# Two stretches of projections behind every second step of both attentions, in place of one behind each step

## The reference

```python
def first_block(x, ...):
    h = rms_norm(x, attn_norm)
    x = x + hybrid_mixer(h, ...)      # proj = h @ w_in: q_f, k_f, v_f, forget gate, q_s, k_s, v_s, two gates
    h = rms_norm(x, ffn_norm)
    x = x + hier_moe(h, ...)          # 64 experts, 2 per token
    return rms_norm(x, final_norm)

# hybrid_mixer: two attentions of 8 heads of 64 features
o_f = fox_attention(q_f, k_f, v_f, log_f)       # causal, plus cumulated log forget gates
o_s = swa_sink_attention(rotary(q_s), rotary(k_s), v_s, sinks)   # window of 128, one sink per head
merged = sigmoid(gl_f + b) * (o_f @ w_proj_fox) + sigmoid(gl_s + b) * (o_s @ w_proj_swa)
return merged @ w_out

# second_block, its mixer: retention of 4 heads and latent attention (MLA) of 8 heads, 96 features for q and k
ret_out = silu(rg) * head_groupnorm(retention(rq, rk, rv))
mla_out = mla_causal(q, k, v)
return concatenate([ret_out, mla_out]) @ w_o    # then the gated feed-forward of 2816 and the last gate
```

## Time and profile before

| what | us |
|---|---|
| median of 3 runs | 2106.96 (2105.54 to 2107.35) |
| the profiled execution | 2105.58 |
| its span, first to last instruction | 2103.8 |
| TensorE busy, whole span | 1805.8 (86%) |
| VectorE busy | 778.0 (37%) |
| ScalarE busy | 694.2 (33%) |
| mean granted clock | 0.95 |

### The profile page before, as it was taken

How to read it: one execution, slowest core, us unless ns; L and a number is a source line. 1 busy time by engine, 2 the same in 40 slices (tenths; PEclk the granted TensorE clock), 3 DMA queues, 4 the chain that set the end, 5 groups by cost and what they waited for, 6 DMA issues and landing times.

```text
span 2103.8 us, 35728 instructions
## 1 busy us (share of the span) xinstructions
PE 1805.8 (86%) x14374; PEld 1232.2 (59%) x14374; DVE 778.0 (37%) x1481; ACT 694.2 (33%) x1292; POOL 77.6 (4%) x184
## 2 busy tenths in 40 slices
PE   7999999787877768777877778699979899999988
PEld 5677787543434434343433434378757788788866
DVE  4555425632222222222222222445455633332254
ACT  4444422232222232223222232432555422222151
POOL 0000000000000000000000002410000000000000
PEclk9999999898999999999999999899989999999999
DMA  6222233599999999999999999742221132324211
GB/s 202 76 81 81 61 100 103 216 410 425 427 426 426 426 426 427 425 428 426 427 426 425 427 425 427 288 120 76 67 85 51 61 99 81 109 91 140 100 61 40
DMA packets 108451, 505.95 MB, mean 240 GB/s; under 512 B 9400, under 2 KB 58808, under 8 KB 75104
## 3 DMA queue, kind: packets, MB, share of 16 engines
q1 hardware_dynamic: 99744, 490.49, 58.4%
q10 hardware_dynamic: 7520, 11.37, 2.0%
q0 software_dynamic: 1120, 3.16, 0.5%
HBM read 497.31 MB, written 2.11 MB: 237 GB/s over the span
## 4 chain that ended last, share of the span: by engine, by line
PE 59%; DMA 29%; DVE 7%; ACT 3%; issue 2%; SPq 1%; ACTq 0%; DVEq 0%
DMA ring<-in_w 28%; PE bank L609 13%; PE bank L610 12%; PE bank L611 12%; PE bank L2131 8%; PE bank L2043 4%; PE bank L2122 3%; PE bank L773 2%; DVE w_lo L707 2%; ACT w_hi L694 1%; PE bank L799 1%; PE bank L785 1%; SPq L1716 1%; DMA raw<-in_w_in 1%; PE bank L1096 0%
## 5 line engine op out<-in xcount | busy, mean ns | idle before, releaser
L2131 PE MATMUL bank<-ring,XTs 128*32 128x256 f32 x4096 | 287.2, 428 | 113.9 <-DMA ring<-in_w 110.4
L2369 DVE TENSOR_TENSOR x<-x,bank 128x512 f32<-128x512 f32 x264 | 163.8, 681 | 486.5 <-PE bank L2122 486.5
L609 PE MATMUL bank<-hTh,w_hi 128*128 128x512 f32 x714 | 288.1, 404 | 13.5 <-DVE w_lo L707 6.7
L2131 PEld LDWEIGHTS bank<-ring,XTs 128*32 128x32 f32 x4096 | 142.8, 120 | 259.4 <-issue 201.5
L707 DVE TENSOR_TENSOR w_lo<-raw,w_hi 128x2048 fp32r<-128x2048 f32 (+3 forms) x85 | 183.1, 2158 | 299.2 <-ACT w_hi L694 299.1
L610 PE MATMUL bank<-hTh,w_lo 128*128 128x512 f32 x714 | 283.7, 397 | 0.0
L611 PE MATMUL bank<-hTl,w_hi 128*128 128x512 f32 x714 | 282.8, 396 | 0.0
L694 ACT ACTIVATE w_hi<-raw 128x2048 fp32r<-128x2048 f32 (+3 forms) x85 | 152.9, 1805 | 173.2 <-PE bank L611 170.3
L2140 PE MATMUL bank<-ring,aT 128*32 128x256 f32 x2048 | 126.9, 389 | 89.5 <-DVE aT L2389 89.5
L1918 ACT ACTIVATE y<-bank 32x256 f32<-32x256 f32 x256 | 95.9, 375 | 226.9 <-PE bank L2122 139.9
L609 PEld LDWEIGHTS bank<-hTh,w_hi 128*128 128x128 f32 x714 | 136.2, 191 | 55.5 <-DVE w_lo L707 17.6
(11 more groups left out here) (375 smaller groups left out, 2249.5 us busy)
## 6 DMA issues: line engine op xcount, KB each, us to landing
ring<-in_w SPq DMA_DIRECT2D x192, 2048.0 KB, 19.6
raw<-in_w_in SPq DMA_DIRECT2D x25, 1024.0 KB, 5.5
raw<-in_w_gate SPq DMA_DIRECT2D x11, 1024.0 KB, 5.3
raw<-in_w_up SPq DMA_DIRECT2D x11, 1024.0 KB, 5.3
raw<-in_w_down SPq DMA_DIRECT2D x11, 1024.0 KB, 4.9
raw<-in_w_out SPq DMA_DIRECT2D x4, 1024.0 KB, 5.1
raw<-in_w_o SPq DMA_DIRECT2D x4, 1024.0 KB, 5.2
raw<-in_w_ple_gate SPq DMA_DIRECT2D x4, 1024.0 KB, 5.1
```

The source lines that it names most:

```text
L609: pe.matmul(dst, left[0], right[0], start=start, stop=False)
L2131: mm = pe.matmul(Hb[BLK * j:BLK * (j + 1), :], XTs[u][:, 4 * (c % 2) + 2 * h + c // 2, :], w[:, at_:at_ + Q], start=(h == 0 and c == 0), s ...
L2369: ins = v.tensor_tensor(xs, xs, Sb[t % 2][n][:, :], ALU.add)
```

## The change

A helper `every_second` wraps a generator: `between(t)` takes nothing behind even steps and two stretches behind odd ones. All six calls use it, three engines in each attention. No instruction is added or taken away. What the steps and the generators issue is the same; the generator's rest is still drained behind the attention.

```diff
+        def every_second(stretches):
+
+            def between(t):
+                if t % 2:
+                    for _ in range(2):
+                        next(stretches, None)
+            return between
...
             stretches = pe_between()
-            pe_attention(pe, MLA, lambda t: next(stretches, None))
+            pe_attention(pe, MLA, every_second(stretches))
...
             stretches = dve_between()
-            dve_attention(v, MLA, chain, lambda t: next(stretches, None))
+            dve_attention(v, MLA, chain, every_second(stretches))
...
             stretches = act_between()
-            act_attention(act, MLA, lambda t: next(stretches, None))
+            act_attention(act, MLA, every_second(stretches))
...
             stretches = act_between()
-            act_attention(act, ATT, lambda t: next(stretches, None))
+            act_attention(act, ATT, every_second(stretches))
...
-            pe_attention(pe, ATT, lambda t: next(stretches, None))
+            pe_attention(pe, ATT, every_second(stretches))
...
             stretches = dve_between()
-            dve_attention(v, ATT, chain, lambda t: next(stretches, None))
+            dve_attention(v, ATT, chain, every_second(stretches))
```

## The result

The changed kernel takes 2117.91 us (median of 5 runs, 2116.65 to 2119.34) against 2106.93 of the kernel before on the same chip. The ratio is 1.0055, with a 95% interval of 1.0044 to 1.0066: 11.0 us slower, where 9.0 were forecast. A second series of the same kernel, run with the experiments, gave 2117.70 and 1.0055 [1.0041, 1.0068].

The account below looks back on a forecast made before the run. TensorE was taken to bound both attentions, with no waits before the change. First attention 8.3 less 2.9 is +5.4 us, second +3.6; +9.0 in all gives 2116.0 us, 0.43% slower, range 2108.6 to 2124.

Parts of the forecast that it names:

- Bank waits: First attention: three projection stretches wait for banks whose copies stand behind a split on ScalarE; 1.5, 1.3 and 1.15, together 3.95 us.
- Start: First attention's start: step 1's scores, without a stretch ahead, wait for step 0's minimum; 0.85 us, less the first merge 0.65.
- Pairs (i2, i3): First attention, third and fourth steps of a head pair: transposes 0.3 us late in the window, 1.2; forgetting scores late, 0.4.
- Step i0 behind a split: First attention, a head pair's first step: VectorE's low half delays the minimum, later transposes are 0.2 or 0.35 late; 1.1 us.
- Tail: First attention's end: the last step's transposes have no stretch ahead and their scaling stands behind a delayed chain; 1.0 us lost.
- Merges: Both attentions: joining two stretches saves TensorE a switch, 0.20 or 0.10 us each; 2.9 us saved in the first, 0.7 second.
- Latent start: Second attention's start: scores of step 1 wait for the minimum, then run at half clock; 2.5 us, lower bound 0.3.
- Step 10: Second attention, its only split: the later low half on VectorE delays scores and transposes of following steps; 2.2 us.
- Rival A: Both attentions: only small stalls, no net change, as switches could be free; +2.2 us, 2109.2; chance 0.15.
- Rival C: First attention: deeper chain through both helpers, each of eight splits costs 2.2 us; 12.5 us more, 2128.5; chance 0.10.
- Rival B: Both attentions: faster, a merged pair saves 0.86 us, deciding from 0.62; -5.6 us, 2101.4; chance 0.05.
- Rival D: Many short stalls lower TensorE's clock, 2.4 us lost per fall; four falls cost 9.6 us more, 2125.6; chance 0.08.

## Why the prediction was right, step by step

- **What bounds it.** Right. TensorE had no slack in either attention, and every wait moved the end: 6.55 + 4.63 = 11.2 us of stages against 11.1 between the profiled executions, with 0.1 net outside them.
- **Bank waits, 3.95.** Right: 1.50, 1.30 and 1.10 are 3.90, at the three stretches named. Turning the copies round removes these three waits.
- **Start, 0.65.** 0.90. S(1) starts 1.54 us behind S(0), where 1.35 was worked out. The step that was left out is VectorE's: M(0) cannot begin before the low half ahead of it is done.

```profile
74.07 2.29 DVE L715 TENSOR_TENSOR w_lo<-raw,w_hi 128x2048 fp32r<-128x2048 f32 x1 [1.40 <-ACT w_hi L702]
...
76.34 0.34 DVE L869 CUSTOM_DVE_ANT_0 scratch<-bank,cst,small 128x128 f32<-128x128 f32 x1
```

M(0) begins 0.76 us behind S(0) at 75.58; before, where VectorE was free, it was 0.52. In other traces it is up to 1.1, with waits of S(1) up to 1.41: this wait depends on when S(0) meets the low half.
- **Pairs (i2, i3), 1.2 + 0.4.** Right where such a pair is an ordinary one: +0.13 with a merge of 0.21 in it is 0.34 a pair in the window (the rows have it as 0.18 at S and 0.17 at T, where the prediction had all of it at T), -0.08 against -0.21 is 0.13 in the forgetting attention.
- **What failed here: the covers V(-1) and V(15).** The prediction laid out one ordinary pair and applied it to all, the first ones too. At step 2 there is no V yet, so S(3) stands 0.59 us earlier behind S(2) and waits 0.70 for M(2). At step 18 V is that of step 15, a window step of 8 matmuls where the forgetting attention has 16 (0.66 us busy against 1.09), so S(19) waits 0.49. At the latent step 2 it is S(3) again, 0.53. Together 1.7 us by the brackets that no term had. The sentence on the second attention that ordinary pairs have no wait was right; S(3) isn't in an ordinary one.
- **Step i0 behind a split, 1.1.** 0.93: 0.43 at step 12, 0.25 each at 24 and 28 against the pairs that only merge, and nothing where a bank wait stands ahead, as said. Step 4 shows none. In the second trace step 12 has 0.23 and the sum is 0.73; the waits there are the same, and what differs is the stretch of 256-column matmuls behind them.
- **Tail, 1.0.** T(31) waits 0.70, +0.61.
- **Merges, 2.9 and 0.7.** In the first attention right, 0.21 a pair of 512 columns. The 0.12 for a pair of 256 columns has no clean row: -0.22 at steps 16, 17, and -0.30 at 12, 13 in the kernel of the gaining pairs, with lengths that vary by 0.2. In the latent attention a merge brings nothing: V to S has a surcharge there. S of 256 columns takes 0.97 behind V (1575.47 to 1576.44 in the changed kernel), where it took 0.86 behind a stretch (1567.88 to 1568.74 before), and that eats the 0.10 of a merge.

```profile
1575.47 1.13 PE L781 MATMUL bank<-arena 96*128 96x256 f32 x4
1576.44 1.04 PE L793 MATMUL bank<-cst,arena 128*128 128x128 f32 x8
...
1567.88 1.03 PE L773 MATMUL bank<-arena 96*128 96x256 f32 x4
1568.74 1.04 PE L785 MATMUL bank<-cst,arena 128*128 128x128 f32 x8
```

The prediction took 0 for this switch in both attentions; it is 0 in the first (S of 256 has a pitch of 0.63 both ways) and 0.10 in the second. The 0.43 and the 0.33 of the prediction are two measures of the same first matmul: the chain counts from end to end (and has 0.43 in the latent attention too), the timeline from start to start (0.34 in the first). By starts, the 0.21 is some 0.12 at a stretch's first matmul and 0.09 at its last, which takes 0.32 ahead of these scores; ahead of the latent scores it takes 0.23, as inside a stretch.
- **Latent start, 2.5.** 2.47 (2.2 in the second trace), and the twenty matmuls show that the clock is its cause: at full clock S(1) with its stretches takes 2.2 us less. The spell at half clock was 4.4 us behind S(1), where 4.8 were taken over.
- **Step 10, 2.2.** 1.86. The waits in brackets are 0.30, 0.43, 0.53 at S(12), T(10), S(13); in pitches these are late by 0.46, 0.67 and 0.60, where 0.55, 0.7 and 0.6 were written. T(11) is late by less than 0.1, where 0.2 to 0.3 were.
- **Rival A**, small stalls, falls: all of the waits named are there. **Rival C**, 2.2 for every split, falls: pairs with a split and without a bank wait lose 0.2 to 0.43. **Rival B** falls with 0.21 a pair. **Rival D** is not the cause: the clock was 1.00 all through the first attention in both traces of the changed kernel, and in the latent one the only spell at half clock is that of its start. But its mechanism is not far off. In two of the eight traces that have waits of 1.0 us or more in the first attention, those of the copies ahead of the high half and of the twenty more matmuls, one such wait was followed by a spell of half clock that cost 1.6 us. The Trainium skill, "TensorE: Matmul & The Clock Gate", section "A second HAM failure mode: psum-queue depth-cycling", describes a clock that swings between its levels where TensorE idles briefly and often between groups of matmuls. Those two traces agree in part, with one swing each and not a series; the other six show none.
- The sum was within 2.0 us of the measured difference, and the range held it. In part that is luck, since misses of both signs met. In the latent attention S(3) (0.77 in its pair of steps) and the merges (0.7) were missing 1.5 us, step 10, the tail and the start were 0.4 too dear: 4.63 in place of 3.6. In the first, the covers (1.2 by the brackets, 1.0 beyond what such pairs lose anyway) and the start (0.25) were missing, and the tail and step i0 were 0.6 too dear in this trace; the rest, 0.4 together, are small: 6.55 in place of 5.4.

## What to carry to other kernels

Before work that fills is moved away from a step, ask for each answer of a helper what TensorE still has between the question and the use, and ask it for the first steps, the last, and the seam between two kinds of work separately: there the cover is thinner than in the steady part. Look at the helpers' lists as well, which needn't be moved with those of the engine that they serve: left in place, they took 5.4 of the 6.55 us in the first attention away, and a third of the whole loss, 3.9 us, came from short copies that ended up behind a split of 1.9 us on ScalarE. Where the bound engine has no idle time a merge is worth the surcharge of one switch, here 0.2 us, and nothing where the new neighbours have a surcharge of their own. Turning the copies round got 2.4 of the 3.9 back, because the split itself then came later.

## What the runs showed of the hardware

- Waits of 1.0 to 1.5 us of TensorE were followed by half clock in 2 of 8 traces, once each, for about 3.5 us. The same wait of 1.30 us in the same place was followed by full clock in the four other traces that have it.
- After an idle spell of 2.85 us the clock was 0.50 from S(0) at 1554.24 on, while twenty matmuls kept TensorE busy, and 1.00 in 1562 to 1566. In this one trace a wait filled with idle work gave the clock back ahead of the work that counts.
- The idle spell ahead of the latent S(0) had either clock behind it, and not by its length: S(0) took 0.68 us in seven traces behind 3.04 to 3.73 us (in the changed kernel the granted clock was 1.00 there), 1.19 in two behind 2.74 and 2.85, and 0.90 to 1.20 in three behind 4.0.
- The switch from values (weights of 64 columns) to scores costs nothing in the first attention, whose scores use 64 rows (0.63 us both ways), and 0.10 us in the latent one, whose scores use 96 (0.97 for 0.86). A stretch's last matmul takes 0.32 ahead of the former and 0.23 ahead of the latter. Whether the rows are the cause was not tried.
- From the end of ScalarE's copy to the stretch that waits for its bank it was 0.15 us (109.01 to 109.16).
